# Causal mask of the prompt attention moved from TensorE into VectorE's pass over the score banks, with three PSUM banks and two positions rearranged

## What is computed

```
a = gelu(z[:, :2*D_A]);  u = a[:, :D_A];  va = rmsnorm(a[:, D_A:], av_g)
s_a = einsum('hts,bcshd->bcthd', ws_m, vc) + bs            # gating mix of one 128-row tile
...
s = einsum('bqhmd,bkhmd->bhmqk', q, k) * ATTN_SCALE          # m = 0, 1: two score maps per head
s = where(kpos <= qpos, s, NEG_INF);  p = softmax(s)
o_b = einsum(p[m=0] - lam * p[m=1], v)
out = concat([u * s_a, rmsnorm(o_b, on_g) * (1 - lam_init)]) @ w_out
```

## Time and profile before

| | us |
|---|---|
| median of 3 runs | 1022.73 |
| lowest and highest of them | 1018.94, 1022.89 |
| the profiled execution, device time | 1022.66 |
| its span, first to last instruction | 1020.8 |
| TensorE's busy time in it | 962.5 |
| VectorE's busy time in it | 440.4 |
| the 120 us that hold the attention pipeline of layer 0, TensorE busy | 117.02 |
| the same of layer 1 | 117.05 |

### The profile page before, as it was taken

One profiled execution on the slowest core, in us unless ns is written; L12 is line 12 of the kernel. 1 busy time (PEld: TensorE's weight loads), 2 busy tenths in 40 slices (PEclk: granted clock), 3 DMA queues, 4 the chain that ended last, 5 costly groups with the idle time before them and its releaser, 6 DMA issues.

```text
span 1020.8 us, 13578 instructions
## 1 busy us (share of the span) xinstructions
PE 962.5 (94%) x4918; PEld 495.4 (49%) x4918; DVE 440.4 (43%) x1154; ACT 233.3 (23%) x483; POOL 191.5 (19%) x265
## 2 busy tenths in 40 slices
PE   6999999999998999999599999999989989999991
PEld 4444455556456444434254344655555554444340
DVE  2403122566346466551343111345563565555523
ACT  2101255542001011111121114555220011111110
POOL 2333201331101111111125031022220011111100
PEclk9999999999998999999899999999999999999996
DMA  8716003342511979998742150134252059799946
GB/s 335 267 31 257 1 1 129 103 146 91 220 42 63 383 259 370 420 421 328 240 144 83 49 209 1 68 109 160 63 208 103 21 222 367 274 381 412 403 153 209
DMA packets 39769, 197.72 MB, mean 194 GB/s; under 512 B 7632, under 2 KB 7760, under 8 KB 23824
## 3 DMA queue, kind: packets, MB, share of 16 engines
q1 hardware_dynamic: 19744, 136.22, 34.0%
q0 software_dynamic: 15888, 45.87, 12.8%
q10 hardware_dynamic: 4064, 14.68, 4.0%
HBM read 177.35 MB, written 29.88 MB: 203 GB/s over the span
## 4 chain that ended last, share of the span: by engine, by line
PE 84%; DVE 6%; DMA 4%; issue 2%; POOL 1%; ACT 1%; POOLq 0%; SPq 0%; ACTq 0%; DVEq 0%
PE ps L673 77%; PE ps L671 6%; DMA cat<-y_rows 1%; DMA x<-in_xp 1%; POOL st L517 1%; PE ps L688 1%; DMA y_rows<-hn,isca 1%; DVE cat L1720 1%; DVE hT L1393 0%; DMA hT<-h_rows,igat 0%; DVE tmp L1542 0%; DVE st L1543 0%; ACT hn L1306 0%; DVE st L1510 0%; DVE o_sb L1530 0%
## 5 line engine op out<-in xcount | busy, mean ns | idle before, releaser
L673 PE MATMUL ps<-ring,hT 128*128 128x512 f32 (+2 forms) x1056 | 382.4, 595 | 2.9 <-DVE hT L1393 2.5
L673 PEld LDWEIGHTS ps<-ring,hT 128*128 128x128 f32 (+2 forms) x1056 | 148.9, 166 | 198.1 <-issue 196.9
L673 PE MATMUL ps<-ring,cat 128*128 128x512 f32 (+2 forms) x560 | 195.4, 596 | 2.6 <-ACT hn L1306 2.4
L673 PEld LDWEIGHTS ps<-ring,cat 128*128 128x128 f32 (+2 forms) x560 | 72.9, 162 | 82.3 <-issue 79.4
L617 POOL DMA_INDIRECT y_rows<-hn,isca x28 | 28.1, 1003 | 250.1 <-ACT hn L1306 219.5
L673 PE MATMUL ps<-hT,ring 128*128 128x512 f32 (+1 forms) x256 | 71.8, 437 | 0.3 <-ACT cat L1194 0.3
L515 POOL TENSOR_SCALAR st<-st 128x1 f32<-128x1 f32 (+3 forms) x60 | 16.3, 272 | 282.2 <-ACT sqj L1150 106.4
L517 POOL TENSOR_TENSOR st<-st,half 128x1 f32<-128x1 f32 (+3 forms) x60 | 62.5, 1042 | 11.6 <-POOL st L515 11.1
L1861 DVE TENSOR_TENSOR hT<-ps,par 128x512 f32<-128x512 f32 x56 | 36.0, 685 | 56.0 <-PE ps L671 55.6
L1414 DVE TENSOR_REDUCE st<-sqj 128x8 f32<-128x512 f32 x20 | 13.5, 681 | 108.3 <-ACT sqj L1165 108.2
L1306 ACT COPY hn<-ps 128x1024 f32<-128x1024 f32 x28 | 28.4, 1013 | 118.3 <-PE ps L673 118.3
(11 more groups left out here) (249 smaller groups left out, 1172.7 us busy)
## 6 DMA issues: line engine op xcount, KB each, us to landing
ring<-in_w SPq DMA_DIRECT2D x82, 1024.0 KB
kc<-in_w SPq DMA_DIRECT2D x12, 1024.0 KB
vc<-in_w SPq DMA_DIRECT2D x10, 1024.0 KB
v<-in_w SPq DMA_DIRECT2D x10, 1024.0 KB
kva<-in_w SPq DMA_DIRECT2D x10, 1024.0 KB
kc<-in_ck POOLq DMA_DIRECT2D x32, 256.0 KB, 3.6
vc<-in_cv POOLq DMA_DIRECT2D x32, 256.0 KB, 3.2
h_rows<-qk ACTq DMA_DIRECT2D x10, 512.0 KB, 2.6
```

The lines of the kernel that those rows point to most:

```text
L673: ins = pe.matmul(out, lhsT, rhs, start=start, stop=stop, skip_group_check=loose)
```

## The change

1. The four mask matmuls of each pair are gone, and the second score matmul raises `full_S`. In `biggest(n)` VectorE first adds the mask to the two diagonal blocks, in place in the S bank (128 partitions by 2 times 128 columns, bf16 mask broadcast over the maps), waits for that and then takes the maximum. The swapped copies of the constants are gone too: the bf16 constants shrink from 1408 to 1152 columns (one load at the start of 704 KB, and one cast).
2. Banks: the gating mix of tile 3 (step 16) goes to `spare_turn(16)`, which is T1, where it was in F. The turned heads of tiles 0 and 1 (steps 9 and 13) go to T1, where they were in T0. Tile 2's stay in T0.
3. ScalarE's order in steps 5, 9, 13 and 17: `probs_turned` stands before `sample_turned` and `probs`, where it stood behind both.
4. `turn_out(3)` is put between the matmuls of `out_rows(1)` at (1, 2), where it was at (1, 1). On VectorE `scaled(0)` stands before `head_turned(3)`.

```diff
-        OT = {t: spare_turn(4 * t + 9) if t < TP - 1 else f"T{t % 2}" for t in range(NT)}
+        OT = {0: "T1", 1: "T1", 2: "T0", TP - 1: "T1", TP: "T0"}
+        MIX_IN = {t: "F" for t in range(NT)}
+        MIX_IN[TP - 1] = spare_turn([n for n, works in SMALL.items() if ("mix", TP - 1) in works][0])
...
                 def mix(t):
-                    claim("F")
+                    u = MIX_IN[t]
+                    claim(u)
...
-                        mm(bank(u, m)[:, 0:(i + 1) * P], qT[m * DK:(m + 1) * DK, h, here], kT[m * DK:(m + 1) * DK, h, 0:(i + 1) * P])
-                    for stay, move in ((B_ID, B_CAUSAL), (B_SWAP, B_SWAP_CAUSAL)):
-                        for m in range(2):
-                            r = slice(m * DK, (m + 1) * DK)
-                            mm(bank(u, m)[:, here], c16[r, stay], c16[r, move], start=False, loose=True,
-                               inc=full[u].inc("s", n) if (m == 1 and stay == B_SWAP) else None)
+                        mm(bank(u, m)[:, 0:(i + 1) * P], qT[m * DK:(m + 1) * DK, h, here], kT[m * DK:(m + 1) * DK, h, 0:(i + 1) * P],
+                           inc=full[u].inc("s", n) if m else None)
...
-                    if (n, k) == (1, 1):
+                    if (n, k) == (1, 2):
                         turn_out(TP - 1)
...
                 for n in range(STEPS):
+                    if n in PT_STEPS:
+                        probs_turned(n - 2)
...
-                    if 2 <= n < len(ATT) + 2:
+                    if 2 <= n < len(ATT) + 2 and n not in PT_STEPS:
                         probs_turned(n - 2)
...
                     b0 = FIRST[f"S{n % 2}"]
+                    diagonal = ps[:, b0:b0 + 2, i * P:(i + 1) * P]
+                    link(vec.tensor_tensor(diagonal, diagonal, across(c16[:, B_CAUSAL], 2, P), ALU.add))
                     link(vec.tensor_reduce(stat["mx"][:, c:c + 2], ps[:, b0:b0 + 2, 0:(i + 1) * P], AX.X, ALU.max))
...
+                scaled(0)
                 head_turned(TP - 1)
-                scaled(0)
```

More of the change, by code:

```diff
@@ L77 @@
 B_ID, B_CAUSAL = slice(0, P), slice(P, 2 * P)
-B_SWAP, B_SWAP_CAUSAL = slice(2 * P, 3 * P), slice(3 * P, 4 * P)
 PAIRS = NB // 2
@@ L85 @@
 NSLOT = len(SLOTS)
-B_SAMPLE = slice(4 * P, 4 * P + PAIRS * P)
-B_ONES, B_BEFORE, B_FOLD = (slice((4 + PAIRS + i) * P, (5 + PAIRS + i) * P) for i in range(3))
-NC16 = (7 + PAIRS) * P
+B_SAMPLE = slice(2 * P, 2 * P + PAIRS * P)
+B_ONES, B_BEFORE, B_FOLD = (slice((2 + PAIRS + i) * P, (3 + PAIRS + i) * P) for i in range(3))
+NC16 = (5 + PAIRS) * P
 class Count:
@@ L799, in mix @@
                         r = (h % 2) * DHA
-                        mm(bank("F")[r:r + DHA, (h // 2) * P:(h // 2 + 1) * P][:, at], kva[:, t, h * DHA:(h + 1) * DHA],
-                           ws[:, h, at], inc=full["F"].inc("mix", t) if h == HA - 1 else None)
+                        mm(bank(u)[r:r + DHA, (h // 2) * P:(h // 2 + 1) * P][:, at], kva[:, t, h * DHA:(h + 1) * DHA],
+                           ws[:, h, at], inc=full[u].inc("mix", t) if h == HA - 1 else None)
                 def sample_mix():
@@ L1487, in mix @@
                 def mix(t):
-                    dve.wait_ge(*full["F"].at("mix", t))
+                    u = MIX_IN[t]
+                    dve.wait_ge(*full[u].at("mix", t))
                     bs = par[:, PAR["bs"]].rearrange("p (c t) -> p c t", c=4)
                     n = NROW if t == TP else P
-                    s, o = (a.rearrange("p (c t) -> p c t", c=4)[:, :, P - n:P] for a in (bank("F"), tmp[:, :]))
+                    s, o = (a.rearrange("p (c t) -> p c t", c=4)[:, :, P - n:P] for a in (bank(u), tmp[:, :]))
                     bs = bs[:, :, 0:n]
@@ L1500, in mix @@
                         dve.wait_ge(*dve_s.at("mix", t - 1))
-                    vec.tensor_tensor(added, part, bs, ALU.add).then_inc(*read["F"].inc("mix", t))
-                    dve.wait_ge(*read["F"].at("mix", t))
+                    vec.tensor_tensor(added, part, bs, ALU.add).then_inc(*read[u].inc("mix", t))
+                    dve.wait_ge(*read[u].at("mix", t))
                     vec.tensor_tensor(catT[:, 0:4, t * P:t * P + n], o, catT[:, 0:4, t * P:t * P + n], ALU.mult).then_inc(*dve_s.inc("mix", t))
@@ L2016, in layout @@
     c16[:, B_BEFORE] = r[:, None] < r[None, :]
-    swapped = (r + P // 2) % P
-    c16[:, B_SWAP] = np.eye(P)[swapped]
-    c16[:, B_SWAP_CAUSAL] = c16[:, B_CAUSAL][swapped]
     row, key = np.arange(32), np.arange(64)
```

## The result

The changed kernel takes 1024.32 us (median of 10 runs, 1020.99 to 1025.39) where the kernel before, run beside it, takes 1021.19 (10 runs, 1018.94 to 1022.89). The ratio is 1.0030, with a 95% interval of 1.0017 to 1.0043: slower by some 3 us. That is less than the 0.5% that was called the same, and it lies inside the range, but I had forecast 1.1 us less and not 3 more. The 1021.6 of the forecast counts from the first three runs of the kernel before (1022.73); its ten runs give 1021.19, so that a time near 1021.6 would have been no gain either. The profiled execution took 1024.4 us with a span of 1022.5.

The account below looks back on a forecast made before the run. TensorE, busy 962.5 of 1020.8 us, was taken as the bound. Per layer -1.68 + 0.92 - 0.76 + 1.8 - 0.79 = -0.5 us, two layers -1.0, from 1022.66 to 1021.6 us; range 1015.5 to 1025.

Parts of the forecast that it names:

- c: Price of one mask add in VectorE's queue: 0.46 us, bounds 0.20 and 0.73, entering three times per layer.
- rival D: Slower: an in-place add in PSUM costs much more than one to SBUF; at 1.5 us each, 1027.9 us; chance 0.04.
- Steps 8 and 12: VectorE's queue sets when F is free, so the add delays the large piece by 0.46 us each, +0.92 a layer.
- rival C: The adds are hidden at steps 7, 8, 11 and 12: 3.5 us less in all, 1018.1 us; chance 0.06.
- The waits of step 10 and of the tail: Turned heads in T1 remove step 10's wait, -0.76 us; another eighth of the projection covers the tail's, -0.79, per layer.
- The mix moved to T1: Step 16: the fourth mix waits for ScalarE's copy of pair 13 instead of the sample exponentials, gaining 0.1 us, not 1.74.
- rival B: T1 is not the new wait, because tile 3's mix is read in time: 3.6 us less, 1018.0 us; chance 0.09.
- the new wait: turn_probs(15) waits for VectorE to read the mix from T1, starting about 245.8, not 244.00; steps 15 to 17 cost +1.8 us.
- The mask's price: Four mask matmuls follow one another on TensorE, 0.21 us a set; 8 sets come off per layer, 1.68 us.
- Rival E: The mask is not taken off TensorE's list at all, scores to transposes unchanged: +3.4 us, 1025.0 us; chance 0.04.
- their own results ready: Sample transposes, small wsS matmul and weigh(14), queued behind turn_probs(15), wait for nothing else, so its delay passes on whole.
- the shift passes through: After the attention TensorE's list is the chain again, so two layers' -1.0 us goes straight into the time.

Follow-up runs that it names:

- moves_only: The changed kernel's banks and orders, with the masks as matmuls on TensorE as in the kernel before; ratio 1.0004 against the kernel before.
- after_busy: The changed kernel with 8 and 9 unread fp32 identity matmuls filling TensorE's two waits of steps 16 and 17; 1019.26 us, ratio 0.9997 against the kernel before.
- mask_twice: The kernel before with the four mask matmuls of every pair issued twice; 1021.23 us, ratio 1.0005.
- after_mix_s0: The changed kernel with the fourth mix in bank S0 in place of T1; 1021.54 us, ratio 1.0014 against the kernel before.
- after_first: after_mix_s0 with VectorE's order turned at steps 7, 11, 15 and 16, where TensorE waits for it; 1012.50 us, ratio 0.9937 against the kernel before.
- moves_first: Order and banks of after_first, with the masks as matmuls on TensorE again; 1013.31 us, ratio 0.9938 against the kernel before.
- before_first: The kernel before, banks and masks unchanged, with only VectorE's order turned as in after_first; 1016.49 us, ratio 0.9963.
- masks_split: moves_first with the masks as VectorE adds for ten pairs and as matmuls for six; 1011.18 us, ratio 0.9910 against the kernel before.
- after_again: The changed kernel measured once more, nothing altered; 1023.07 us, ratio 1.0029 against the kernel before.
- mask_only: The kernel before with only the mask moved to VectorE, banks and orders as before; 1024.92 us, ratio 1.0043.
- after_mix_f: The changed kernel with the fourth mix back in bank F; 1019.04 us, ratio 0.9986 against the kernel before.
- adds_twice: after_mix_s0 with every mask add done twice on VectorE; 1024.88 us in one run.

## Why the prediction was wrong, step by step

At full clock the sum can be closed, with layer 1 after against layer 1 before.

**Right.** The add: all 32 take 422 to 433 ns (median 427), and the maximum starts 0.46 us after it, in step 15 of layer 0:

```profile
237.02 0.43 DVE L1512 TENSOR_TENSOR ps<-ps,c 128x256 f32<-128x256 f32 x1
237.48 1.22 DVE L1513 TENSOR_REDUCE st<-ps 128x2 f32<-128x1024 f32 x1
```

c = 0.46, as taken from the earlier trace rows; rival D is out. Steps 8 and 12: the large piece of step 8 stands 0.52 us later against step 6's than before, that of step 12 0.46 later against step 10's (forecast 0.46 each), so rival C is out. The waits of step 10 and of the tail are gone; from `weigh(15)` to `turn_out(4)`, behind the tail, it is 0.86 us less (forecast 0.79). The mix moved to T1 gained 0.12 (forecast 0.1), and from the mix to `turn_probs(15)` it is 3.93 us (744.38 to 748.31 in layer 1) where it was 2.02 (241.98 to 244.00), 1.9 more, as the forecast start at 245.8 asked for; so rival B is out: the new wait is there, ended by the line that was named.

**The mask's price.** "The row decides, and I use 0.21": this step failed, and so did "The four matmuls thus follow one another", since a set measures 0.11. The distance from the start of the masks to the start of the transposes was read as the masks' own, but 0.10 of it stays when they go. With 7 masks in the stretch that is 0.7 us a layer; with step 0's, 0.8, or 1.6 in all. Rival E, which gave the masks no worth at all, was half right.

**A small term the other way.** I said that the work behind `turn_probs(15)` has "their own results ready". Before, the sample transposes start 0.66 us behind `turn_probs(15)` (244.00 to 244.66), since they wait for VectorE's fold; after, 0.47 (748.31 to 748.78), since the fold has long been there. With a like 0.1 at the next piece, 0.3 us of the 1.8 was absorbed.

Stretch: forecast -7 x 0.21 + 0.92 - 0.76 + 1.8 = +0.49; with 0.7 more for the masks and 0.3 less for the fold, +0.89; measured 109.38 - 108.49 = +0.89. With the tail (-0.86) and step 0 (-0.11) a layer comes to -0.1, two to -0.2 where the forecast had -1.0. At full clock the change does next to nothing.

**The clock.** The rest, some 3 us, is the term that wasn't there, and it is the step that decided. The sum goes from the layers straight to the time, "so the shift passes through": it took every instruction of TensorE at the length of the rows at full clock. It forecast about 1.7 us of idle time, some 2 us of matmuls and another wait of nearly 2 where there had been one wait of 1.74, and stopped at their sum. Of 4 profiled layers of the changed kernel 2 show the fall, at 3.7 and 3.1 us; none of the 18 of before, moves_only, after_busy, mask_twice, after_mix_s0, after_first, moves_first, before_first and masks_split do. after_busy, which fills both waits and moves nothing else, gives 3.3 us back. That the clock falls for the idle time in steps 16 and 17 is thereby shown. Not shown is which wait sets it off: in layer 0 after, it fell ahead of the second one, behind a wait like that of the kernel before, and a kernel with 1.16 and 1.76 us kept full clock in both layers. Open too is why the fall comes in one layer and not in the other, with waits equal to 0.02 us (after_again), and how much of the differences between runs is clock lost in the routing stage behind the attention, where most of the profiles show a fall in one layer or both (before: 0.50 from 316 to 320 us).

## What to carry to other kernels

Cost a new wait on the bounding engine twice: its length, and what the clock may take behind it (here 1.2 to 3.7 us where it fell, for waits of 1.2 to 2.3 us). A full clock there in one profile doesn't mean that it holds in every execution: compare the mean granted clock of all of them. Read the price of an instruction from the interval across it with and without a like one, not from the distance to the next start: what follows may need that distance anyway. And when a half-idle engine holds up the busy one, turn its order before moving work on to it or off it: here the order was worth 4 us on the kernel before, and with the new banks 9 between the medians, 5.5 of them in the stretches; the place of the mask, once the order was right, 0 to 2.

## What the runs showed of the hardware

- With waits of 1.74 us and 1.3 to 1.8 us, and 2 us of matmuls between them, the granted clock went from 1.00 to 0.50 in 2 of 4 layers, for 7 and 10 us; in one of them ahead of the second wait. One wait of 2.31 us did so in one of two layers of mask_only and of after_mix_f, with 1.2 and 1.3 us lost, and waits of 1.18 and 1.38 us in one of two of adds_twice. One of 1.74 us alone (before), and 1.16 and 1.76 us (moves_only), did not in two layers each. Matmuls that no one reads, put into the waits, kept it at 1.00. In four of the five falls TensorE was at work when the clock went down, 1.1 to 1.6 us behind a wait.
- Four bf16 mask matmuls in two row groups cost 0.11 us; the passage from 64-row to 128-row matmuls 0.10 us with or without them (step 6, layer 0, of three kernels).
- An in-place add of 256 fp32 columns in PSUM with a bf16 operand takes VectorE 427 ns (median of 32), no more than one that reads PSUM and writes SBUF (0.42 us). The Trainium skill (VectorE: DVE Perf Modes, The TRN2 errata) gives (N + 151) / 0.96 ns for fp32 adds, by which I estimate 424 ns for N = 256: the trace agrees.
